# Projection in four overlapped token parts, with first loads of two stages issued one stage earlier

## The chip, the cores and the metric

The kernel runs on one core of a Trainium2 chip. The metric is the device time of one execution in microseconds; a comparison goes by the median of several runs. TensorE (PE in the profile) multiplies, ScalarE (ACT), VectorE (DVE) and GpSimd (POOL) do the rest, and SyncE (SP) issues nearly all DMA transfers in the order of its program.

## The reference, cut to what matters

One inference step of a two-layer decoder over 2048 prompt tokens and 32 sample tokens (8 sequences of 4), width 1024:

```
x          -> pool_layer: rmsnorm, w_in_a, causal window means, w_map_a, silu gate, w_out_a, residual   (x1)
k, v       =  rmsnorm(x1, norm_kv_g) @ w_kv                  # 1024 -> 2048, both are also outputs
q, z       =  rmsnorm(x1, norm_b_g) @ w_in_b                 # 1024 -> 2048
o          =  softmax(q0 k0) v - lam * softmax(q1 k1) v      # 8 heads, ALiBi, causal
y          =  rmsnorm(x1 + (rmsnorm(o) * silu(z)) @ w_out_b)
```
The sample tokens attend to 1024 cached positions as well. Everything is float32.

## The kernel before, in words

The program runs in stages, each a block of its own behind a barrier of all engines: `setup`, `PoolLayer`, `OutLayer` (x1), `project` for tokens 0 to 1023, `project` for tokens 1024 to 2079, `attention` (prompt), `sample_attention`, `last_layer`. Float32 products are made of three matmuls on operands split into a high and a low part (`three`, L295 to L297).

**OutLayer** (L653) splits the weights in eight chunks while TensorE multiplies its first two token blocks; `load_g` (L670) fetches the gated input of block n+2 only when block n has been added up and stored (`step`, L709).

**project** (L808) has eight *units* of weights, each 1024 x 512, in the order v, k, q, z, v, k, q, z; a unit is used by eight *steps* (nine in the second half), one for each 128 tokens, or for a q unit one for each 128 channels by 512 tokens. A step is 24 matmuls. Before the units, the blocks of 128 tokens are normalized: ScalarE squares (L205) and takes the root (L211), VectorE averages (L224) and scales (L230, L233), TensorE turns the block with eight transposes (L253), ScalarE and VectorE split it (`high` L268, `low` L273). Each engine carries out its list in order. The points to follow:

- SP issues the weights of unit u+1 at the start of its list for unit u (L911, `load`, L885), which it reaches after the stores of the last step of unit u-1.
- ScalarE and VectorE split those weights (L949, L981, `split`) at the start of their lists for unit u, ahead of all evictions of unit u. They wait there until the weights have landed.
- Rows of v and k are copied out by VectorE (L986), z goes through Silu on ScalarE (L968), q is split by both (L959, L993).
- A k block is also turned: `turn_keys` (L1024) puts four transposes (L1032) on TensorE two steps later (`LATE = 2`), out of the copied rows; ScalarE and VectorE then split them as well (L959, L993). There are `NR = 3` PSUM banks for these transposes, shared with the norm's, so a turn waits only for the split of the third key block before it (L1030). The products rotate over five PSUM banks, `NS = 5`.

**attention** (L1064) starts with loads of head 0 (L1148): keys and queries in high and low form, in two groups. TensorE waits for the first group before its first score (L1218) and for the second before the second pair of query blocks. GpSimd meanwhile makes the bias tile (L1193 to L1197) that VectorE needs for its first score reduction (L1343). In the profile's rows the output layer's first operand buffers are `early_loads`, the projections' normalized input is `b_x_hi` and `b_x_lo`.

## Time and profile before

| | us |
|---|---|
| median of 3 runs | 3381.88 (3379.08 to 3382.13) |
| profiled execution | 3381.49 |
| its span, first to last instruction | 3379.7 |
| TensorE busy | 3126.8 (93%) |
| VectorE busy | 1581.0 (47%) |
| ScalarE busy | 1188.3 (35%) |
| mean granted TensorE clock | 0.962 of full |

Stages on TensorE by their first and last product: pooling layer until 970, output layer 988 to 1375, first projection 1401 to 1764, second 1792 to 2206, prompt attention 2223 to about 2880, then sample attention and the last layer. Busy time of TensorE is the sum of its matmuls' durations without overlap counted twice; the time between products is what a stage's start or a wait costs. Times of rows are microseconds from the start of the span.

### The profile page before, as it was taken

How to read it: one execution, taken by the hardware profiler on the slowest of the kernel's cores; microseconds unless marked ns; L12 is line 12 of the kernel's file. 1: busy time of each engine (PE TensorE's matmuls, PEld its weight loads, DVE VectorE, ACT ScalarE, POOL GpSimd, SP SyncE). 2: the span in 40 equal slices, each digit the busy share in tenths (PEclk: the TensorE clock that was granted, in tenths of full speed). 3: DMA queues.
4: the chain of work that ended last, by engine and by line, in shares of the span. 5: the costliest groups of instructions: out<-in, count | busy, mean ns of one | idle time of the engine just before them, and what ended most of it. 6: DMA issues, size and time to landing. Idle time of an engine off the chain costs nothing. (4 is left out here: it accounts for less than half of the span.)

```text
span 3379.7 us, 44652 instructions
## 1 busy us (share of the span) xinstructions
PE 3126.8 (93%) x17000; PEld 2582.6 (76%) x17000; DVE 1581.0 (47%) x2673; ACT 1188.3 (35%) x2149; POOL 95.8 (3%) x109
## 2 busy tenths in 40 slices
PE   5999999999978999799988999969999999787598
PEld 4888888889977888588876777749999999543486
DVE  4574655564641111331214312148888888332464
ACT  3333333342320000322113221137777777332222
POOL 0000000000000000000000000010000000000111
PEclk8999999999989999899998999979999999998799
DMA  4434343424233222343324423282445451686453
GB/s 138 137 106 137 106 137 106 139 100 170 83 106 98 90 93 86 120 144 127 128 101 138 138 102 116 93 185 54 111 103 112 103 110 30 263 309 234 168 177 115
DMA packets 249951, 431.96 MB, mean 128 GB/s; under 512 B 20889, under 2 KB 119961, under 8 KB 244217
## 3 DMA queue, kind: packets, MB, share of 16 engines
q1 hardware_dynamic: 249775, 429.59, 40.0%
q8 instruction: 114, 1.87, 0.3%
q14 instruction: 62, 0.50, 0.1%
HBM read 327.30 MB, written 102.95 MB: 127 GB/s over the span
## 5 line engine op out<-in xcount | busy, mean ns | idle before, releaser
L295 PE MATMUL proj_acc<-proj_w_hi,b_x_hi 128*128 128x512 f32 (+1 forms) x832 | 330.0, 397 | 0.0
L297 PE MATMUL proj_acc<-proj_w_hi,b_x_lo 128*128 128x512 f32 (+1 forms) x832 | 326.5, 392 | 0.0
L296 PE MATMUL proj_acc<-proj_w_lo,b_x_hi 128*128 128x512 f32 (+1 forms) x832 | 326.0, 392 | 0.0
L1290 ACT ACTIVATE attn_scores<-attn_scores,attn_lowest 128x1024 f32<-128x1024 f32 (+15 forms) x256 | 307.2, 1204 | 28.8 <-DVE attn_lowest L1343 28.8
L1230 PE MATMUL attn_s<-attn_k_hi_lo,attn_q_lo_hi 128*128 128x512 f32 (+3 forms) x640 | 266.3, 416 | 33.0 <-DMA attn_q_hi_lo<-qT_lo 28.6
L1260 PE MATMUL attn_o<-attn_v,attn_aT 128*128 128x128 f32 x2176 | 295.6, 276 | 1.0 <-ACT attn_aT L1301 1.0
L1260 PEld LDWEIGHTS attn_o<-attn_v,attn_aT 128*128 128x128 f32 x2176 | 279.4, 191 | 10.6 <-ACT attn_aT L1301 1.2
L1343 DVE CUSTOM_DVE_ANT_0 attn_scores<-attn_s,attn_bias 128x1024 f32<-128x1024 f32 (+7 forms) x256 | 216.7, 856 | 151.1 <-PE attn_s L1231 118.3
L295 PE MATMUL pool_acc<-pool_odd_x_hi,pool_wh 128*128 128x272 f32 (+1 forms) x768 | 249.1, 324 | 0.0
L296 PE MATMUL pool_acc<-pool_odd_x_lo,pool_wh 128*128 128x272 f32 (+1 forms) x768 | 248.5, 324 | 0.0
L297 PE MATMUL pool_acc<-pool_odd_x_hi,pool_wl 128*128 128x272 f32 (+1 forms) x768 | 248.3, 323 | 0.0
L295 PE MATMUL outa_acc<-outa_w_hi,outa_g_hi 128*128 128x512 f32 (+1 forms) x544 | 213.9, 393 | 29.2 <-DVE outa_w_lo L764 18.0
L1231 PE MATMUL attn_s<-attn_k_hi_lo,attn_q_hi_lo 128*128 128x512 f32 (+3 forms) x640 | 229.4, 369 | 0.0
L296 PE MATMUL outa_acc<-outa_w_lo,outa_g_hi 128*128 128x512 f32 (+1 forms) x544 | 213.5, 392 | 0.0
L297 PE MATMUL outa_acc<-outa_w_hi,outa_g_lo 128*128 128x512 f32 (+1 forms) x544 | 213.4, 392 | 0.0
L295 PE MATMUL pool_acc<-even_x,pool_wh 128*128 128x512 f32 x512 | 203.6, 398 | 1.4 <-DVE even_x L273 1.4
L297 PE MATMUL pool_acc<-even_x,pool_wl 128*128 128x512 f32 x512 | 201.7, 394 | 0.0
L296 PE MATMUL pool_acc<-even_x,pool_wh 128*128 128x512 f32 x512 | 200.2, 391 | 0.0
L297 PEld LDWEIGHTS proj_acc<-proj_w_hi,b_x_lo 128*128 128x128 f32 (+1 forms) x832 | 151.5, 182 | 40.2
L296 PEld LDWEIGHTS proj_acc<-proj_w_lo,b_x_hi 128*128 128x128 f32 (+1 forms) x832 | 151.9, 183 | 38.4
L295 PEld LDWEIGHTS proj_acc<-proj_w_hi,b_x_hi 128*128 128x128 f32 (+1 forms) x832 | 151.8, 182 | 37.9
L1301 ACT ACTIVATE attn_aT<-attn_t 128x512 f32<-128x512 f32 (+3 forms) x320 | 164.8, 533 | 42.2 <-PE attn_t L1244 39.4
(223 smaller groups left out, 5833.8 us busy)
## 6 DMA issues: line engine op xcount, KB each, us to landing
pool_wu<-in_w_in_a SPq DMA_DIRECT2D x16, 2048.0 KB, 7.8
pool_wz<-in_w_in_a SPq DMA_DIRECT2D x16, 2048.0 KB, 7.7
smp_k_page<-in_cache_k SPq DMA_DIRECT2D x64, 512.0 KB, 5.4
smp_v_page<-in_cache_v SPq DMA_DIRECT2D x64, 512.0 KB, 5.6
pool_wm<-in_w_map_a SPq DMA_DIRECT2D x16, 1024.0 KB, 5.6
early_loads<-gatedT SPq DMA_DIRECT2D x16, 1024.0 KB, 5.9
proj_wst<-in_w_kv SPq DMA_DIRECT2D x8, 2048.0 KB, 9.4
proj_wst<-in_w_in_b SPq DMA_DIRECT2D x8, 2048.0 KB, 8.3
```

The costliest lines, as they stand in the source:

```text
L295: pe.matmul(out, ah, bh, start=first, stop=False)
L296: pe.matmul(out, ah, bl, start=False, stop=False)
L297: return pe.matmul(out, al, bh, start=False, stop=last)
L1230: pe.matmul(out[:, o:o + w], qx[a][:, c, q], keys, start=True, stop=False)
L1231: last = pe.matmul(out[:, o:o + w], qs[a][:, c, q], keys, start=False, stop=True)
L1260: last = pe.matmul(o_ps[r], at[idx % NAT][:, kb % QUAD, :], v[h % 2][:, kb, :], start=kb == 0, stop=kb == n - 1)
L1290: act.activation(part, part, ACT.Exp, scale=-1.0, bias=low[s][:, x:x + 1], accum_out=sums[s][:, i:i + 1]).then_inc(expd, 1)
L1301: act.activation(at[idx % NAT][:, 0:n, :], t_ps[idx % 2][:, 0:n, :], ACT.Copy).then_inc(taken, 1)
L1343: dve.tensor_tensor_reduce(sc[s][:, c, a0:a0 + n], s_ps[idx % 2][:, 0:n], bias[h % 2][:, b0:b0 + n], -SCALE, low[s][:, x - 2:x - 1] if x > ...
```

## The change

There is one `Project` instead of two calls of `project`. Its 2080 tokens come in four parts (512, 512, 512, 544). Each part goes through all eight units, so there are 32 units of four steps (five in the last part), and each of the 32 loads and splits its 2 MB of weights. The normalized input alternates between two buffers: the blocks of part p+1 are normalized during units 1 to 4 (1 to 5 before the last part) of part p, one a unit, with square at step 0, root and scale at step 1, the eight transposes after step 2, `high` and `low` at step 3. The norm has two PSUM banks, the keys one, `key_bank`; a turn of keys waits for the split of the key block just before it. OutLayer fetches its gated input two blocks earlier and issues the first weights (`nxt.load_w`) and the first rows of x1 of the projection. In the last part, at the start of unit 5, SP issues four loads of head 0 (`FirstHead.first_loads`); attention then waits for those and for two smaller ones.

```
+                if i in (3, 4):
+                    sp.wait_ge(g_lo, i - 2)
+                    load_g(sp, i - 1, i - 3, P)
...
+                if ahead:
+                    sp.wait_ge(g_lo, 2 * i + s + 3)
+                    load_g(sp, 2 * i + s + 4, s, ahead)
+                if x_n:
                     sp.wait_ge(out_sem[s], 16 * i + 16)
-                    load_x(2 * i + s + 2, s, n)
-
-            with sp.Fori(0, pairs - 1) as i:
-                step(i, 0, P)
-                step(i, 1, P)
-            step(pairs - 1, 0, rest)
-            step(pairs - 1, 1, 0)
+                    load_x(2 * i + s + 2, s, x_n)
+
+            step(0, 0, P, P, P)
+            sp.wait_ge(w_lo, KC // LK)
+            nxt.load_w(sp, 0)
+            step(0, 1, P, P, P)
+            with sp.Fori(1, pairs - 2) as i:
+                step(i, 0, P, P, P)
+                step(i, 1, P, P, P)
+            step(pairs - 2, 0, P, rest, P)
+            step(pairs - 2, 1, P, 0, P)
+            sp.dma_start(nxt.slots[0][:, :], D["x1"][0:P, :]).then_inc(nxt.row_sem, 16)
+            step(pairs - 1, 0, P, 0, rest)
+            step(pairs - 1, 1, P, 0, 0)
...
+        self.slots, self.x, self.turn_banks = [slot], [], []
+        self.row_sem = m.sem("row_in")
...
+        NS, NR = 5, 3
+        LATE = 2
...
+        self.turn_banks += [m.ps(f"turn{i}", [P, KC // 2, P]) for i in range(2)]
+        key_bank = m.ps("turn_keys", [P, CT, P])
...
+        steps = [(p, u, b) for p in range(PN) for u in range(NUN) for b in range(first_block[p + 1] - first_block[p])]
+        def late_keys(n):
+
+            return n - LATE if n >= LATE and kind(n - LATE) == "k" and whole(n - LATE) else None
...
+        def norm_block(p, u):
+
+            if p + 1 == PN or not 1 <= u <= first_block[p + 2] - first_block[p + 1]:
+                return None
+            return first_block[p + 1] + u - 1
...
+            norm.load(sp, 1)
+            norm.load(sp, 2)
+            self.load_w(sp, 1)
+            norm.load(sp, 3)
+            for n, (p, u, b) in enumerate(steps):
+                w = p * NUN + u
+                if b == 0 and w >= 1 and w + 1 < NWU:
+                    sp.wait_ge(lo, w * KC)
+                    self.load_w(sp, w + 1)
+                if b == 0:
+                    c = norm_block(p, u + 1)
+                    if c is not None:
+                        norm.load(sp, c)
+                if p == PN - 1 and u == NUN // 2 + 1 and b == 0:
+
+                    done = max(d for x, d in t_index.items() if steps[x][0] < p or steps[x][1] < NUN // 2)
+                    for s in range(NR):
+                        sp.wait_ge(t_out[s], 32 * len(range(s, done + 1, NR)))
+                    sp.wait_ge(mm, step_at[PN - 1, 0, 0])
+                    nxt.first_loads(sp)
+                if transposed(n):
+                    store_turned(n)
+                else:
+                    store_rows(n)
+                late = late_keys(n)
+                if late is not None:
+                    store_turned(late)
...
+            def split(w):
+                gain = gains[units[w % NUN][1][3]]
+                act.wait_ge(w_sem[w % 2], 16 * (w // 2) + 16)
+                if w >= 2:
+                    act.wait_ge(mm, step_at[(w - 1) // NUN, (w - 1) % NUN, 0])
...
+            two_ahead(first_block[1], lambda b: norm.moments(act, b), lambda b: norm.high(act, b), lambda: split(0))
+            for n, (p, u, b) in enumerate(steps):
+                w = p * NUN + u
+                if b == 0 and w + 1 < NWU:
+                    split(w + 1)
+                if kind(n) == "z":
+                    r, a = take(act, n)
+                    act.activation(r, a, ACT.Silu).then_inc(taken_act, 1)
+                if transposed(n):
+                    turned_high(n)
+                late = late_keys(n)
+                if late is not None:
+                    turned_high(late)
+                c = norm_block(p, u)
+                if c is not None and b == 0:
+                    norm.square(act, c)
+                if c is not None and b == 1:
+                    norm.root(act, c)
+                if c is not None and b == 3:
+                    norm.high(act, c)
...
+            AHEAD = 2
+            def turn_keys(n):
+                i = k_index[n]
+                wait_taken(pe, n)
+                if i >= 1:
+                    pe.wait_ge(t_lo, t_index[by_k[i - 1]] + 1)
+                    last = pe.transpose(key_bank[:, j, :], res[n % NS][:, j * P:(j + 1) * P], K["ident"][:, :])
+            for n, (p, u, b) in enumerate(steps):
+                w = p * NUN + u
+                if b == 0:
+                    pe.wait_ge(lo, w * KC + KC)
+                if u == 0:
+                    c = first_block[p] + b if p == 0 else first_block[p + 1] - 1
+                    if p == 0 or b == 0:
+                        pe.wait_ge(norm.lo, 2 * c + 2)
+                if n >= NS:
+                    wait_taken(pe, n - NS)
+                w_hi, w_lo = wh[w % 2], wl[w % 2]
+                xh, xl = self.x[p % 2]
+                a = acc[n % NS]
+                rn = tokens(p, b)[1]
+                for k in range(KC):
+                    if transposed(n):
+                        ch = slice(b * P, (b + 1) * P)
+                        last = three(pe, a[:, :], w_hi[:, k, ch], w_lo[:, k, ch], xh[:, k, 0:CN], xl[:, k, 0:CN],
+                                     k == 0, k == KC - 1)
+                    else:
+                        tok = slice(b * P, b * P + rn)
+                        last = three(pe, a[0:rn, :], xh[:, k, tok], xl[:, k, tok], w_hi[:, k, :], w_lo[:, k, :],
+                                     k == 0, k == KC - 1)
+                last.then_inc(mm, 1)
+                late = late_keys(n)
+                if late is not None:
+                    turn_keys(late)
+                if n + AHEAD < first_block[1]:
+                    norm.turn(pe, n + AHEAD)
+                c = norm_block(p, u)
+                if c is not None and b == 2:
+                    norm.turn(pe, c)
...
+    def first_loads(self, sp):
+        HD = self.HD
+        for name, dst, top, bottom in (("kT", self.kk, "hi", "lo"), ("qT", self.qx, "lo", "hi")):
+            for part, rows in ((top, slice(0, HD)), (bottom, slice(HD, P))):
+                src = self.D[f"{name}_{part}"][0:P, :].rearrange("(c p) s -> p c s", c=2)
+                sp.dma_start(f32(dst[rows, :, :]), src).then_inc(self.sem, 16)
...
-            for n in range(6):
-                load_kq(0, n, slice(0, (far + 1) * P) if n < 2 else slice(near * P, (far + 1) * P), begin_in)
-            for n in range(6):
-                if n >= 2:
-                    load_kq(0, n, slice(0, near * P), kq_in[0])
+            for n in (4, 5):
+                load_kq(0, n, slice(near * P, (far + 1) * P), begin_in)
+            for n in (4, 5):
+                load_kq(0, n, slice(0, near * P), kq_in[0])
                 load_kq(0, n, slice((far + 1) * P, S), kq_in[0])
...
-                    pe.wait_ge(begin_in, 96)
+                    pe.wait_ge(head0.sem, 64)
+                    pe.wait_ge(begin_in, 32)
...
+            with ExitStack() as middle:
+                proj = Project(nc, middle, D, K, early, slot, parts, x1_blocks, block_at, gains)
+                head0 = FirstHead(nc, back, D, K, S, kq0)
+                with ExitStack() as inner:
+                    out.ctx, out.m.ctx = inner, inner
+                    out.run(proj)
+                even2 = Memory(nc, middle, "even2").sb("x", [P, size], F32R)
+                proj.run(halves(even2), head0)
+            with ExitStack() as hold:
+                Memory(nc, hold, "hold").sb("kq", [P, 4 * S])
+                attention(nc, D, K, S, H, head0, early, slot)
```
The split, the copies and `turned_low` on VectorE are in the same order as on ScalarE. The rest of the diff gives buffers other places and passes them on.

## Rows read from the trace of the kernel before

**Rows 1.** Waits of TensorE over the whole run (us in total, times, longest):
```profile
PE attn_s L1230 <- DMA attn_q_hi_lo<-qT_lo: 28.6, 2, 16.2
...
PE proj_turn L1032 <- DVE proj_res L986: 0.6, 1, 0.6
```
**Rows 2.** Busy time by stretch: length, then PE, PEld, DVE, ACT, POOL, clock, DMA share, GB/s:
```profile
1764.00:1792.00 28.00, 5.28 (x23) 4.49 (x24) 11.93 (x25) 13.69 (x26) 0.00 (x0) 0.56 0.45 166
1792.00:2206.40 414.40, 414.40 (x1843) 321.44 (x1842) 97.89 (x156) 78.58 (x135) 0.00 (x0) 1.00 0.33 113
```
**Rows 3.** Timeline, TensorE and VectorE, third block of the output layer: start, length, [idle before]:
```profile
1045.44 0.79 PE L295 MATMUL outa_acc<-outa_w_hi,outa_g_hi 128*128 128x512 f32 x1 [11.18 <-DVE outa_g_lo L752]
...
1050.72 0.41 PE L295 MATMUL outa_acc<-outa_w_hi,outa_g_hi 128*128 128x512 f32 x1
...
1033.04 1.23 DVE L757 TENSOR_TENSOR outa_x<-outa_acc,outa_x 128x1024 f32<-128x1024 f32 x1 [12.86 <-PE outa_acc L297]
1043.01 2.29 DVE L752 TENSOR_TENSOR outa_g_lo<-early_loads,outa_g_hi 128x2048 fp32r<-128x2048 f32 x1 [8.75 <-ACT outa_g_hi L735]
```
**Rows 4.** Timeline, all engines, start of the first projection:
```profile
1379.97 0.83 SPq L194 DMA_DIRECT2D proj_x<-x  x2
...
1383.77 1.06 ACT L205 ACTIVATE proj_junk<-proj_x 128x1024 f32<-128x1024 f32 x1 [46.45 <-DMA proj_x<-x]
...
1386.24 0.20 ACT L211 ACTIVATE proj_stats<-proj_stats 128x1 f32<-128x1 f32 x1
...
1387.48 2.82 PE L253 MATMUL proj_turn<-all_ident,proj_x 128*128 128x128 f32 x12 [12.37 <-DVE proj_x L233]
...
1390.11 5.02 ACT L949 ACTIVATE proj_w_hi<-proj_wst,all_gain_kv 128x512 fp32r<-128x512 f32 x8 [2.20 <-DMA proj_wst<-in_w_kv]
...
1397.49 1.28 DVE L273 TENSOR_TENSOR b_x_lo<-proj_turn,b_x_hi 128x512 fp32r<-128x512 f32 x2
...
1401.48 0.78 PE L295 MATMUL proj_acc<-proj_w_hi,b_x_hi 128*128 128x512 f32 x1
```
**Rows 5.** Timeline of TensorE, second projection: one block's eight transposes among products:
```profile
1799.10 1.03 PE L253 MATMUL proj_turn<-all_ident,proj_x 128*128 128x128 f32 x8
```
**Rows 6.** Timelines of VectorE and ScalarE, first k unit:
```profile
1450.16 0.69 DVE L986 COPY proj_res<-proj_acc 128x512 f32<-128x512 f32 x1 [4.75 <-PE proj_acc L297]
...
1466.32 1.88 DVE L986 COPY proj_res<-proj_acc 128x512 f32<-128x512 f32 x3
...
1460.26 5.04 ACT L949 ACTIVATE proj_w_hi<-proj_wst,all_gain_b 128x512 fp32r<-128x512 f32 x8 [20.87 <-DMA proj_wst<-in_w_in_b]
```
**Rows 7.** Timelines of VectorE, SyncE and ScalarE, first q unit:
```profile
1496.94 0.69 DVE L986 COPY proj_res<-proj_acc 128x512 f32<-128x512 f32 x1 [4.17 <-PE proj_acc L297]
...
1514.89 0.69 DVE L993 TENSOR_TENSOR proj_turned_lo<-proj_turn,proj_turned_hi 128x512 fp32r<-128x512 f32 x1 [0.21 <-DVE proj_turned_lo L993]
...
1499.68 0.57 SPq L885 DMA_DIRECT2D proj_wst<-in_w_in_b  x1
...
1507.92 5.03 ACT L949 ACTIVATE proj_w_hi<-proj_wst,all_gain_b 128x512 fp32r<-128x512 f32 x8 [9.94 <-DMA proj_wst<-in_w_in_b]
```
**Rows 8.** Timeline of ScalarE, first z unit:
```profile
1541.94 0.60 ACT L959 ACTIVATE proj_turned_hi<-proj_acc 128x512 fp32r<-128x512 f32 x1 [4.84 <-PE proj_acc L297]
1553.62 5.03 ACT L949 ACTIVATE proj_w_hi<-proj_wst,all_gain_kv 128x512 fp32r<-128x512 f32 x8 [11.08 <-DMA proj_wst<-in_w_kv]
1558.68 1.28 ACT L968 ACT_TABLE_LOAD   x1
1559.97 1.58 ACT L968 ACTIVATE proj_res<-proj_acc 128x512 f32<-128x512 f32 x3
```
**Rows 9.** Timeline, GpSimd and VectorE, start of prompt attention:
```profile
2219.87 1.89 POOL L1197 TENSOR_SCALAR_AFFINE_SELECT attn_bias<-attn_bias 128x2048 f32<-128x2048 f32 x1
...
2224.85 1.23 DVE L1343 CUSTOM_DVE_ANT_0 attn_scores<-attn_s,attn_bias 128x1024 f32<-128x1024 f32 x1 [67.72 <-PE attn_s L1231]
...
2246.03 1.09 DVE L1343 CUSTOM_DVE_ANT_0 attn_scores<-attn_s,attn_bias 128x896 f32<-128x896 f32 x1 [13.39 <-PE attn_s L1231]
```

More of the change, by code:

```diff
@@ L842, in project @@
-        per = [full // 4] * 4 + [1]
-        norm = Norm(m, blocks, K["ident"], lambda b: (xh, xl, b * P), [m.sb(f"x{i}", [P, KC * P]) for i in range(3)],
-                    m.sb("junk", [P, KC * P]), m.sb("stats", [P, 4 * NB]), turn_ps, None, KC * P)
-        AHEAD = 3
-        LATE = 2
-        def keys_at(n):
-            u, b = divmod(n, NB)
-            return (u, b) if n >= 0 and units[u][1][0] == "k" and b < full else None
-        def transposed(u, b):
-            return units[u][1][0] == "q" and b < full
@@ L922, in _, with store_rows @@
-            for s in range(NS if rest else NS - 1):
+            def store_rows(n):
+                p, u, b = steps[n]
+                i, name = units[u][0], kind(n)
+                cols = slice(i * CN, (i + 1) * CN)
+                r0, rn = tokens(p, b)
+                if name in "kv":
+                    dst = D[name + "_prompt"][r0:r0 + rn, cols] if whole(n) else D[name + "_sample"][:, cols]
+                else:
+                    dst = D[name + "_rows"][r0:r0 + rn, cols]
+                wait_taken(sp, n)
+                sp.dma_start(dst, res[n % NS][0:rn, :]).then_inc(out_sem[n % NS], 16)
@@ L923, in _ @@
+            for s in range(NS):
                 sp.wait_ge(out_sem[s], 16 * stores[s])
@@ L999, in after @@
[L999 to L1001 removed]
+                    dve.sem_inc(taken_dve, 1)
             norm.clear(dve)
[L1004 to L1015 removed]
+            two_ahead(first_block[1], lambda b: norm.scale(dve, b), lambda b: norm.low(dve, b), lambda: split(0))
@@ L1070, in attention @@
+def attention(nc, D, K, S, H, head0, early, slot):
     NB = S // P
@@ L1995, in program @@
-        attention(nc, D, K, S, H)
+        gains = [K["gain_kv"], K["gain_b"]]
+        x1_blocks = [(D["x1"][b * P:(b + 1) * P, :], P) for b in range(S // P)] + [(D["x1"][S:NT, :], R)]
+        H = D["cache_k"].shape[2]
+        K["HD"] = D["lambda_q1"].shape[1]
+        size = 2 * KC * part
+        halves = lambda t: [t[:, i * KC * part:(i + 1) * KC * part].rearrange("p (k t) -> p k t", k=KC) for i in range(2)]
+        with ExitStack() as below:
+            even = Memory(nc, below, "even").sb("x", [P, size], F32R)
```

365 lines of the change are left out of this document (158 added, 207 removed).

## The prediction

> **What bounds the kernel now.** I read the page's busy times first: TensorE is busy 3126.8 of 3379.7 us (93%, table above), every other engine under half, so the time can only come out of TensorE's pauses, or go into new ones. Then TensorE's waits: there are few, and they sit where a stage begins. The largest that the change touches is prompt attention waiting for its keys and queries, 28.6 us in two waits; inside a projection there is just one wait of 0.6 us, for a copied key block [rows 1]. The busy times by stretch say the same: the second projection is 414.4 us with TensorE busy in all of them, and the 28.0 us between the two projections hold 5.28 us of work [rows 2]. So the projections are bound by TensorE and the seams by latency. Last I read the timelines of the seams and of one k, one q and one z unit, to see what stands behind each wait, and how much slack the 45 us of an eight-step unit hide. A step takes 5.44 us: the 4.84 us of idle and 0.60 us of work of a q eviction repeat from step to step [rows 8].
>
> **What goes away.**
> (a) Output layer, third block. TensorE idles 11.18 us for the low half of its gated input, then pays for a fallen clock: its next 12 products take 5.28 us (1045.44 to 1050.72) where 12 at full clock take half a step, 2.7. With the input fetched early, VectorE still has to add up the first block (from 1033.04, 1.23 us) and then split (2.29 us), both ahead of TensorE: 1036.6 instead of 1045.4 [rows 3]. I take 8.9 plus 2.5 = 11.4 us; bounds 0 (the two extra 1 MB loads delay the weight chunks as much) and 13.7. The projection's 2 MB and the row block issued by SP here go at nothing: they lie beside 380 us of products, and without that cover would cost some 8 us, as a 2 MB load does below.
> (b) Start of the projection. Before, both row blocks and the weights are issued behind the barrier at 1379.97; the first block is there at 1383.77, the split of the weights starts at 1390.11, block 0 is ready at 1397.49 + 1.28 = 1398.8 and the first product runs at 1401.48. After, block 0 and the weights are there, block 1 is not: issued at 1379.97, there 3.8 us later, squared and rooted by 1385.5, when the split can start, 4.6 us earlier. Only two blocks are turned ahead of the first product, so it starts some 0.7 us behind block 0 instead of 2.7: 2.0 more. 6.6 us; bounds 0 and 21.5 (all from the barrier to the product) [rows 4].
> (c) Seam between the projections. 28.0 us, 1764.0 to 1792.0, are gone, since no block, barrier or first load stands there [rows 2]. But four more blocks are now turned in TensorE's path (three of that seam, one of the first start), eight transposes or 1.03 us each [rows 5]: 28.0 - 4.1 = 23.9 us. The matmuls themselves are as many as before.
> (d) Start of attention. TensorE's first wait does not shrink by its 16 us: GpSimd's bias chain starts behind the same barrier and ends at 2219.87 + 1.89 = 2221.8, and the first reduction, at 2224.85, needs it. That is late next: gain 3.0. The second wait goes whole, for only 1.8 MB of the second group are left, ahead of all other loads: VectorE's idle of 13.39 us becomes some 0.5, gain 12.9 [rows 9]. 15.9 us; bounds 3 and 28.6 [rows 1].
> Sum of gains: 11.4 + 6.6 + 23.9 + 15.9 = 57.8 us.
>
> **What comes in.** 16 more splits of weights: 128 conversions each on ScalarE and VectorE, at 5.04 / 8 = 0.63 us or so [rows 6], 80 us each. By busy time they are hidden, with both engines at about a quarter in the projection [rows 2]. By order they are not. The split of the next weights stands ahead of all evictions of a unit, on both engines, and waits for a load that SP issues when the unit starts. That stall was there before, and it is as long as before; but the unit around it is now 22 us instead of 45, and two things that TensorE waits for now fall inside it. I count from T, the moment at which the last step of the unit before is evicted, and TensorE would reach the end of step j at T + 5.44 j.
> *q unit, keys.* T = 1496.94; the load is issued at 1499.68, split from 1507.92, and the third key block is split (low half) at 1514.89 + 0.69 = T + 18.6 [rows 7]. The fourth key block is turned after step 2, at T + 10.9 + 0.5 = T + 11.4, and with one key bank that waits for the third block's split. Before, three banks made it wait for the first's only. Wait: 7.3 us. Bounds: 0 if the split were over by T + 11, and 10 if the load, with more transfers around it, lands some 3 us later.
> *k unit.* T = 1450.16; split from T + 10.1 to 15.1 on ScalarE; the first key copy ends at 1466.32 + 0.63, T + 16.9 [rows 6], the transposes need it after step 3, T + 16.3: 0.6 us, the wait that before shows once [rows 1]. With a norm block: square 1.2 to T + 16.3, a table load 1.28 [rows 8] to 17.6, root; from root to the transposes took 1.24 us (1386.24 to 1387.48) [rows 4], so T + 18.9 against 16.3 + 0.5 of key transposes: 2.0 us in all.
> *z unit, norm block.* T = 1541.94; split from 1553.62, T + 11.7, to 16.7; table load for Silu to 18.0, Silu of the first step 0.5, square 1.2, Silu of the second 0.5, T + 20.2; table load for the root to 21.5, and 1.24 more: T + 22.8 against T + 16.3 [rows 4, 8]. Wait: 6.5 us.
> *v unit, norm block.* As the k unit, without keys: T + 18.8 against 16.3, 2.5 us.
> *q unit, norm block.* The root is queued behind the fourth key block's split; with that released at T + 19.2 and up to 3 us more for a buffer still being stored, the block is scaled by about T + 23.5 (an estimate), and TensorE, held up by the keys, arrives at 24.6. Nothing.
> Where the trace shows no such wait, its bounds are 0 and the time from T + 16.3 to the end of the chain plus 3 us for a later load.
> Parts 0 to 2 each: k 2.0, q 7.3, z 6.5, v 2.5, k 0.6, q 7.3, z 0 = 26.2; three parts 78.6. The fifth block of the last part adds 0.9 in a k unit. In the last part, five steps let the third key block be split before the long stall, and there is no norm: only 2 x 0.6. Sum 80.7 us.
> *Clock.* Nine of these waits are 6.5 to 7.3 us long. After the 11.18 us of idle the granted clock was at its lower level, 1.2 GHz, and 2.5 us were lost [rows 3]; beside the wait of 0.6 us it stayed at 1.00 [rows 1, 2]. I take 1.5 us each, 13.5 (bounds 0 and 22.5).
> Loss: 94 us. A wait in one unit does not shorten that of the next, since the next load is issued when the next unit starts.
> The rest is at nothing: norm row loads (0.5 MB a unit) and head 0's four 1 MB loads stand on SP behind the weights' load, the next load comes 27 us later, and the DMA engines are a third in use [rows 2]. Without cover the 4 MB would delay one unit by some 5 us.
>
> **Sum.** 3381.5 (the profiled execution; its span 3379.7 and 1.8 around it; the median is 0.4 more) - 57.8 + 94.2 = 3417.9. Forecast: 3418 us, slower by 1.1%.
>
> **The Trainium skill.** The z unit's row shows the Silu starting 1.29 us after its table load started, straight behind it [rows 8]. The Trainium skill, page "ScalarE: Activation LUTs", section "What ACT_TABLE_LOAD costs", gives about 2.66 us for a switch, 1.28 for the load and 1.38 for a drain; the trace agrees with the first part alone. By the page, each of the four switches in front of a norm block's transposes (one in k, two in z, one in v) would add 1.38 us in three parts, 16.6 us in all, and the sum would be 3434. The rows on the clock are above: 5.28 us for 12 products behind an idle stretch. The Trainium skill, page "TensorE: Matmul & The Clock Gate", section "HAM oscillation — how this bites in real kernels", says that a product loop with recurring idle gaps pays for the slow clock at each gap, not once; this trace has only single gaps, so it cannot show it yet.
>
> **Rivals.**
> *A, the waits don't show.* Faster: the weights' load overtakes, because SP reaches it earlier than I count or the transfer is shorter, so splits are over by T + 11. Then only the gains count: 3381.5 - 57.8 = 3324. It decides from a load issued some 7 us earlier. Against: in the q unit SP issues it 2.7 us behind T and the split starts at T + 11.0, in the k and z units at T + 10.1 and 11.7 [rows 6 to 8]; nothing in the change moves the issue within the unit. Chance 0.13.
> *B, only the key bank costs.* The norm blocks' chain is shorter than its parts added up, or the square runs before the split: 6 x 7.3 + 1.2 + 9 of clock = 54, so 3378, no change. For: the pieces come from different places. Against: ScalarE's order is fixed, and it puts the split first. Chance 0.09.
> *C, contention.* With weights at twice the rate and row blocks beside them, each load lands 2 us later, 20 waits: 40 more, 3458. For: the q unit's load already took 8.2 us, with only stores beside it [rows 7]. Against: 0.33 of the DMA's time in use [rows 2]. Chance 0.05.
> *D, table switches cost double where ScalarE is pressed:* Silu and root in turn cost as much again as the 1.28 us of the row, in front of each norm block's transposes: four switches in three parts, 12 x 1.28 = 15.4 us, 3433. Against: the Silu of the z unit follows its load at once [rows 8]. Chance 0.03. It is the page's rule above.
> *E, the early loads do nothing at attention,* for GpSimd's chain and the second group hold as before: only 12.9 us less gain, 3431; inside the forecast's range. Chance 0.04, counted apart.
>
> **Chances and range.** Forecast 0.62, A 0.13, B 0.09, C 0.05, D 0.03, E 0.04, something else 0.04. A measurement of this kernel can tell about 0.2%, 6.8 us. The forecast's own range comes from the clock (-13.5, +9), attention (-12.7, +12.9), and a microsecond either way in 20 waits, taken together 3393 to 3442. For 8 in 10 it has to take in B: 3372 to 3444; A and C are left out. Slower by over 0.2% (above 3388.6): forecast but a hundredth, C, D, E and some of the rest, 0.76. Within: most of B, 0.08. Faster: A and the rest, 0.16.
>
> **What would show it.** Right: in the projection, TensorE waits at the key transposes for the low half of turned keys, some 7 us, six times; at the norm's transposes for the scaled block, about 6.5 us three times, 2 to 3 us six times; a granted clock that falls again and again between the first and the last product of the projection, a stretch of 860 to 880 us. At the output layer's third block 2.3 us of idle. At attention, VectorE's first reduction 3 us earlier behind the barrier, and no 13 us gap. Wrong: TensorE all but gapless in the projection (A); waits for keys only (B); loads landing over 11 us after issue (C); a gap behind table loads (D). The forecast fails if SP issues the weights well before the stores that I put in front of it, or if TensorE does not stop at the fourth key block.

## The result, and the profile of the changed kernel

| | kernel before | changed kernel |
|---|---|---|
| median of the runs, us | 3381.89 (3379.08 to 3382.13, 4 runs) | 3427.74 (3424.3 to 3434.82, 4 runs) |
| profiled span, us | 3379.7 | 3427.2 |

The changed kernel is slower: its time over that of the kernel before is 1.014, with a 95% interval from 1.0123 to 1.0158. That is 46 us, where 36 were forecast. The two spans differ by 47.5 us.

The page of the changed kernel still shows TensorE as the only busy engine (span, then busy us, share, instructions):
```profile
span 3427.2 us, 44871 instructions
...
PE 3148.3 (92%) x17000; PEld 2593.7 (76%) x17000; DVE 1661.0 (48%) x2800; ACT 1280.6 (37%) x2291; POOL 96.0 (3%) x109
```
The surprise of this page is that TensorE's busy time rose by 21.5 us, from 3126.8, though no matmul was added beside the 32 transposes. Its waits (us in total, times, longest) name where it stands still:
```profile
PE proj_turn_keys L1103 <- DVE proj_turned_lo L1065: 44.3, 6, 8.1
PE proj_turn L253 <- DVE proj_x L233: 19.3, 7, 7.0
PE proj_turn L253 <- DVE region_slot L233: 18.5, 4, 8.8
...
PE attn_s L1332 <- DMA attn_q_hi_lo<-qT_lo: 8.6, 1, 8.6
...
PE attn_s L1332 <- DVE attn_lowest L1445: 6.9, 5, 3.7
PE proj_turn_keys L1103 <- DVE proj_res L1058: 3.5, 5, 1.0
PE outa_acc L295 <- DVE outa_g_lo L763: 3.1, 1, 3.1
```
Of the `region_slot` line, 8.8 us are at the start, ahead of the first product. That leaves in the projection 44.3 us in six waits for the low half of turned keys, 3.5 us in five for a copied key block, and 19.3 + 9.7 = 29.0 us in ten for a scaled norm block: 76.8 us, where the two projections of before had 0.6 [rows 1].

Busy times by stretch (length, then PE, PEld, DVE, ACT, POOL, granted clock, DMA share, GB/s), from SP's first row load behind the barrier to the first product, and from there to the end of the last product:
```profile
1370.39:1385.70 15.31, 3.56 (x16) 3.19 (x17) 10.53 (x23) 12.81 (x24) 0.00 (x0) 0.50 0.63 240
1385.70:2266.70 881.00, 804.14 (x3514) 639.03 (x3512) 285.32 (x454) 262.27 (x433) 0.00 (x0) 0.95 0.46 151
```
The same products with nothing in their way take 779.0 us (first experiment below). So 881.0 us are 779.0 of work, 76.8 of waits, and 804.1 - 779.0 = 25.2 us by which the work is slower, at a mean clock of 0.95. The page counts these 25.2 us as busy.

**Where each part ended up.** Marks of the same events in both traces, in us:

| stretch | before | after | difference |
|---|---|---|---|
| up to SP's first row load of the projection | 1379.97 | 1370.39 | -9.6 |
| from there to the first product | 21.5 | 15.3 | -6.2 |
| first to last product of the projection | 805.0 | 881.0 | +76.0 |
| last product of the projection to the first of the sample attention | 687.9 | 671.1 | -16.8 |
| from there to the first product of the last stage | 267.0 | 270.5 | +3.5 |
| from there to the end | 218.4 | 218.9 | +0.5 |

These differences add up to the 47.5 us, within what rounding leaves. The +3.5 is no part of the change. In the twelve other profiled executions of this case that stretch took between 263.5 and 274.3 us, with the same code.

**Output layer.** TensorE at the third block:
```profile
1036.81 0.79 PE L295 MATMUL outa_acc<-outa_w_hi,outa_g_hi 128*128 128x512 f32 x1 [3.06 <-DVE outa_g_lo L763]
...
1039.53 0.63 PE L295 MATMUL outa_acc<-outa_w_hi,outa_g_hi 128*128 128x512 f32 x1
...
1041.18 0.39 PE L295 MATMUL outa_acc<-outa_w_hi,outa_g_hi 128*128 128x512 f32 x1
```
The block comes at 1036.81 instead of 1045.44, 8.6 us sooner [rows 3]: the pause is 8.1 us shorter (3.06 for 11.18), and the layer's first product came 0.6 us earlier already (987.91 for 988.49). But even a pause of 3.06 us is followed by products of 0.63 us. The twelve products up to 1041.18 take 4.37 us; at full clock they would take 2.7. How long the slow clock stays behind this same pause of 3.06 us differs from execution to execution: in eight of the twelve traces that have it the twelve products take 4.2 to 4.4 us, in the other four, that of experiment 1 among them, 5.28, as long as before behind 11.18 us.

**Start of the projection,** all engines:
```profile
1370.39 0.83 SPq L194 DMA_DIRECT2D proj_x<-x  x2
...
1375.70 5.00 ACT L1014 ACTIVATE proj_w_hi<-region_early,all_gain_kv 128x512 fp32r<-128x512 f32 x8
...
1384.11 1.94 PE L253 MATMUL proj_turn<-all_ident,proj_x 128*128 128x128 f32 x8 [7.80 <-DVE even_x L273]
...
1385.70 0.78 PE L295 MATMUL proj_acc<-proj_w_hi,even_x 128*128 128x512 f32 x1
```
The split starts 5.3 us behind SP's load instead of 10.1, and the first product follows it by 10.0 us instead of 11.4 [rows 4].

**First q unit.** Timelines of VectorE, SyncE, ScalarE and TensorE (T is 1436.2, the last eviction of the k unit):
```profile
1436.23 0.69 DVE L1058 COPY proj_res<-proj_acc 128x512 f32<-128x512 f32 x1 [5.46 <-PE proj_acc L297]
...
1438.98 0.58 SPq L842 DMA_DIRECT2D region_early<-in_w_in_b  x1
...
1448.41 5.01 ACT L1014 ACTIVATE proj_w_hi<-region_early,all_gain_b 128x512 fp32r<-128x512 f32 x8 [10.16 <-DMA region_early<-in_w_in_b]
...
1455.37 0.69 DVE L1065 TENSOR_TENSOR proj_turned_lo<-proj_turn_keys,proj_turned_hi 128x512 fp32r<-128x512 f32 x1 [0.21 <-DVE proj_turned_lo L1065]
...
1456.20 1.09 PE L1103 MATMUL proj_turn_keys<-all_ident,proj_res 128*128 128x128 f32 x4 [8.14 <-DVE proj_turned_lo L1065]
...
1459.22 0.63 PE L297 MATMUL proj_acc<-even_x,proj_w_lo 128*128 128x512 f32 x1
1459.65 0.54 PE L295 MATMUL proj_acc<-even_x,proj_w_hi 128*128 128x512 f32 x1
1460.03 0.39 PE L296 MATMUL proj_acc<-even_x,proj_w_hi 128*128 128x512 f32 x1
```
Read it from the bottom up: TensorE stands 8.14 us at the fourth key block's transposes, for the third block's low half, which VectorE has written at T + 19.8 (T + 18.6 in the prediction's count). That write is so late because the split of the next weights stands ahead of it on both engines, and it starts at T + 12.2 because SP asked for these weights at T + 2.8. After the pause, products take 0.63 us until 1459.65.

**First z unit,** ScalarE, and TensorE's wait:
```profile
1482.09 5.02 ACT L1014 ACTIVATE proj_w_hi<-region_early,all_gain_kv 128x512 fp32r<-128x512 f32 x8 [10.05 <-DMA region_early<-in_w_kv]
1487.12 1.28 ACT L1033 ACT_TABLE_LOAD   x1
1488.42 0.60 ACT L1033 ACTIVATE proj_res<-proj_acc 128x512 f32<-128x512 f32 x1
...
1490.55 1.28 ACT L211 ACT_TABLE_LOAD   x1
1491.85 0.20 ACT L211 ACTIVATE proj_stats<-proj_stats 128x1 f32<-128x1 f32 x1
...
1493.09 1.97 PE L253 MATMUL proj_turn<-all_ident,region_slot 128*128 128x128 f32 x8 [6.35 <-DVE region_slot L233]
```
ScalarE does a split, a table load, Silu, the norm's square, Silu, a table load and the root: the root that scales the norm block stands behind six other pieces of work, each straight behind the one before.

**Start of the prompt attention,** SyncE, GpSimd and VectorE:
```profile
2271.83 0.59 SPq L1250 DMA_DIRECT2D attn_q_hi_lo<-qT_hi  x1
...
2279.37 1.89 POOL L1298 TENSOR_SCALAR_AFFINE_SELECT region_early<-region_early 128x2048 f32<-128x2048 f32 x1
...
2281.48 1.23 DVE L1445 CUSTOM_DVE_ANT_0 attn_scores<-attn_s,region_early 128x1024 f32<-128x1024 f32 x1 [41.85 <-POOL region_early L1298]
...
2289.72 1.09 DVE L1445 CUSTOM_DVE_ANT_0 attn_scores<-attn_s,region_early 128x896 f32<-128x896 f32 x1 [0.89 <-PE attn_s L1333]
```
The first reduction comes 14.8 us behind the last product of the projection, where it was 18.4, and it now waits for GpSimd's bias tile. VectorE's gap of 13.39 us ahead of the second group is one of 0.89 [rows 9].

### The profile page after: what moved, and what is told of

It is laid out like the page before. It is cut to its first block and busy times, and to the rows that moved or that the text cites. A ratio compares the mean times of both kernels' runs of the same rounds, so it can differ in the third digit from the quotient of the medians.

```text
span 3427.2 us, 44871 instructions
## 1 busy us (share of the span) xinstructions
PE 3148.3 (92%) x17000; PEld 2593.7 (76%) x17000; DVE 1661.0 (48%) x2800; ACT 1280.6 (37%) x2291; POOL 96.0 (3%) x109
## 5 line engine op out<-in xcount | busy, mean ns | idle before, releaser
L1445 DVE CUSTOM_DVE_ANT_0 attn_scores<-attn_s,region_early 128x1024 f32<-128x1024 f32 (+7 forms) x256 | 216.7, 856 | 112.0 <-POOL region_early L1298 41.9
L295 PE MATMUL proj_acc<-proj_w_hi,proj_odd_x_hi 128*128 128x512 f32 (+1 forms) x448 | 178.1, 398 | 0.0
L297 PE MATMUL proj_acc<-proj_w_hi,proj_odd_x_lo 128*128 128x512 f32 (+1 forms) x448 | 176.9, 395 | 0.0
L296 PE MATMUL proj_acc<-proj_w_lo,proj_odd_x_hi 128*128 128x512 f32 (+1 forms) x448 | 176.7, 394 | 0.0
L1464 DVE SCALAR_TENSOR_TENSOR attn_scores<-attn_scores,attn_coef 128x1024 f32<-128x1024 f32 (+15 forms) x128 | 173.1, 1352 | 4.5
L1346 PE MATMUL attn_t<-all_ident,attn_scores 128*128 128x128 f32 x1088 | 161.6, 273 | 6.0 <-ACT attn_aT L1403 2.7
L1053 DVE SCALAR_TENSOR_TENSOR proj_w_lo<-region_early,all_gain_kv,proj_w_hi 128x512 fp32r<-128x512 f32 x128 | 86.3, 747 | 162.7 <-ACT proj_w_hi L1014 162.7
L1053 DVE SCALAR_TENSOR_TENSOR proj_w_lo<-region_early,all_gain_b,proj_w_hi 128x512 fp32r<-128x512 f32 x128 | 86.3, 747 | 159.7 <-ACT proj_w_hi L1014 159.7
L295 PE MATMUL proj_acc<-proj_w_hi,even_x 128*128 128x512 f32 x384 | 153.3, 399 | 0.0
L297 PEld LDWEIGHTS pool_acc<-pool_odd_x_hi,pool_wl 128*128 128x128 f32 x768 | 144.3, 188 | 11.8
```

The lines of the kernel that those rows point to most:

```text
L295: pe.matmul(out, ah, bh, start=first, stop=False)
L296: pe.matmul(out, ah, bl, start=False, stop=False)
L297: return pe.matmul(out, al, bh, start=False, stop=last)
L1053: dve.scalar_tensor_tensor(out=wl[w % 2][:, k, :], in0=wst[w % 2][:, k, :], scalar=gain[:, k:k + 1], in1=f32(wh[w % 2][:, k, :]), op0=ALU. ...
L1346: last = pe.transpose(t_ps[idx % 2][:, kb % QUAD, :], sc[u % NSC][:, 0, a0 + kb * P:a0 + (kb + 1) * P], K["ident"][:, :])
L1445: dve.tensor_tensor_reduce(sc[s][:, c, a0:a0 + n], s_ps[idx % 2][:, 0:n], bias[h % 2][:, b0:b0 + n], -SCALE, low[s][:, x - 2:x - 1] if x > ...
```

## The experiments

The theory is that the change loses because a unit is now half as long, while the wait for its weights' load, in front of all evictions on two in-order engines, kept its length; TensorE waits for keys and norm blocks that are queued behind it, and every pause costs clock as well. The rival is that the four overlapped parts cost this by themselves (turning in TensorE's path, one key bank, more transfers), whenever the weights come.

**1. Weights asked for one unit earlier.** Changed kernel with
```diff
-                if b == 0 and w >= 1 and w + 1 < NWU:
-                    sp.wait_ge(lo, w * KC)
-                    self.load_w(sp, w + 1)
+                if b == 0 and w + 2 < NWU:
+                    sp.wait_ge(lo, (w + 1) * KC)
+                    self.load_w(sp, w + 2)
```


> The weights of unit w+2 are issued at the start of unit w, where the changed kernel issues those of w+1; nothing else differs, and as many bytes and conversions are made. Theory (the split of the next weights stands in front of all evictions and waits for a load issued only when the unit starts): the 76.8 us of TensorE's waits inside the projection fall to under 5 us, the clock no longer falls there (some 10 us more), so about 3340 us against 3428, and under the kernel before (3382). Rival (the doubled weights' traffic and conversions slow the stage, wherever they are issued): the same bytes cost the same, 3415 to 3430.

Measured: 3322.07 us (3317.81 to 3322.59), over the kernel before 0.9814 (0.9797 to 0.983). TensorE's stretch, and one split of the first q unit with the load that SP then issues:
```profile
1385.62:2164.58 778.96, 778.96 (x3514) 623.82 (x3512) 287.12 (x454) 262.49 (x433) 0.00 (x0) 1.00 0.51 170
...
1436.44 5.01 ACT L1014 ACTIVATE proj_w_hi<-region_early,all_gain_b 128x512 fp32r<-128x512 f32 x8
...
1437.29 0.56 SPq L842 DMA_DIRECT2D region_early<-in_w_kv  x1
```
Not one wait is left between the first and the last product, and the mean clock is 1.00. The split starts with no wait for a transfer. So overlapped parts, one key bank and 170 GB/s make TensorE wait nowhere by themselves: the rival falls, and all 102.0 us that the projection had lost (881.0 - 779.0) come back when the weights are asked for earlier.

**2. The split moved instead of the load.** On ScalarE and on VectorE, in the changed kernel:
```diff
-                if b == 0 and w + 1 < NWU:
-                    split(w + 1)
...
+                if b == 1 and w + 1 < NWU:
+                    split(w + 1)
```
with the new lines behind the evictions, and the norm's root and scaling, of the second step.

> The loads stand where the changed kernel has them; the split of the next weights stands on ScalarE and VectorE behind the evictions of step 1 of the unit instead of in front of step 0. Theory (it is the order that hurts): waits inside the projection go as with the earlier load, since evictions, key splits and the norm no longer stand behind the load; 76.8 us and the clock, about 3340 us. The split then ends at about T + 18, before the next unit at T + 22. Rival (the load's lateness itself holds TensorE, at the first product of a unit): waits of several us for the low weights in each unit, 3400 us or more.

Measured: 3324.96 us (3316.58 to 3332.75), ratio 0.9822 (0.9798 to 0.9845).
```profile
1384.31:2162.83 778.52, 778.45 (x3514) 623.32 (x3512) 286.04 (x454) 263.26 (x433) 0.00 (x0) 1.00 0.51 171
```
Here the weights come as late as in the changed kernel (8.1 to 10.2 us behind an issue that still stands at the unit's start), but what TensorE needs is no longer queued behind them. The two cures reach the same time. The harm is thus neither the late load nor the early place of the split, but the two together.

**3. The load one step earlier only:** as in 1, but issued at the fourth step of the unit before (`b == 3`).

> The weights of unit w+2 are issued at step 3 of unit w, one step (5.4 us) before the changed kernel issues them, and 16 us later than in the kernel that issues them at the unit's start. Theory (each wait is the lateness of the load, carried through a chain of fixed length): every wait inside the projection is 5.4 us shorter; the key waits of 7.4 us become about 2 (12 us in 6), those in z units about 1 (3 us in 3), the others go: 15 us left of 76.8, PE busy near 780 since such short pauses hardly lower the clock, so 3427 - 62 - 20 = 3345 us. Rival (a threshold: the load must be there before the unit, otherwise the evictions block all the same): 3400 us or more.

Measured: 3333.3 us (3327.15 to 3339.53), ratio 0.9849 (0.9831 to 0.9868). A short wait came up in three places, 5.7 us in all; the stretch from the first to the last product is 788.7 us, so another 4.0 went to slower work:
```profile
PE proj_turn L253 <- DVE region_slot L233: 8.8, 1, 8.8
PE proj_turn L253 <- DVE even_x L273: 7.3, 1, 7.3
PE proj_turn_keys L1103 <- DVE proj_turned_lo L1065: 6.1, 5, 3.0
```
The first two lines are those of the start. By the traces SP issues these loads 5.4 to 6.9 us earlier than in the changed kernel, seen from TensorE's start of the unit (3.0 in the first case, 10 to 12 in the five-step units at the end). Rival A's threshold in the prediction was some 7 us. All but 10 of the 102 us are gained.

**4. A second key bank,** paid for with one accumulator:
```diff
-        NS, NR = 5, 3
+        NS, NR, NKB = 4, 3, 2
...
-                if i >= 1:
-                    pe.wait_ge(t_lo, t_index[by_k[i - 1]] + 1)
+                if i >= NKB:
+                    pe.wait_ge(t_lo, t_index[by_k[i - NKB]] + 1)
```


> Two PSUM banks for the turned keys and four for the products instead of one and five. Theory: the waits of the key transposes for the block before (44.3 us in 6) go to 0, but in the three q units with a norm block the root is queued behind the fourth key block's eviction, and its transposes come up at T + 17 with the block scaled only at about T + 24.8: three new waits of about 7 us. Net about 23 us and some clock: 3400 us. Rival (only the key bank costs, the norm is hidden): 3375 us.

Measured: 3397.74 us (3390.78 to 3399.48), ratio 1.0037 (1.0023 to 1.0051). Waits of TensorE:
```profile
PE proj_turn L253 <- DVE proj_x L233: 32.6, 9, 7.4
PE proj_turn L253 <- DVE region_slot L233: 23.6, 5, 8.8
...
PE proj_turn_keys L1103 <- DVE proj_res L1058: 3.2, 4, 1.3
```
The 44.3 us for keys are gone, and 18.4 of them came back in front of norm blocks (29.0 us before, 32.6 + 23.6 - 8.8 = 47.4 now). The prediction's "nothing" for the norm block of a q unit held only because the key wait in the same unit covered it. No product waits for an accumulator in this trace: every pause of TensorE in the projection stands at a turn. Whether one accumulator and one row buffer less delay the other two engines was not separated.

**5. The norm block turned one step later:**
```diff
-                if c is not None and b == 2:
+                if c is not None and b == 3:
```


> The norm's transposes stand after step 3 of a unit instead of after step 2. Theory: each wait for a scaled block (29.0 us in all, 6.0 to 7.0 in a z unit, 0.8 to 2.2 in k and v units) is shorter by a step of 5.4 us: about 3 us are left in three z units, 26 go, and 3 falls of the clock with them: 3397 us. The key waits stay at 44 us. Rival (the key bank alone costs): no change, 3425 to 3430.

Measured: 3380.99 us (3377.28 to 3385.2, 10 runs), ratio 0.9993 (0.9984 to 1.0003): no difference from the kernel before, and 47 us less than the changed one, from which it differs by one digit.
```profile
1386.08:2222.64 836.56, 794.70 (x3514) 633.58 (x3512) 285.52 (x454) 261.83 (x433) 0.00 (x0) 0.97 0.48 159
...
PE proj_turn_keys L1103 <- DVE proj_turned_lo L1065: 38.9, 6, 7.1
...
PE proj_turn L253 <- DVE proj_x L233: 0.6, 1, 0.6
```
The stage is 44.4 us shorter than in the changed kernel, and the sizes are all in view: norm waits 28.4 less, key waits 5.3, copies 1.4, slower work 9.4 (TensorE busy for 794.7 us instead of 804.1). The expectation missed by 16 us. It had 26 us for the norm waits and some 5 for the clock; it left the key waits as they were and priced the clock at half of what came back.

**6. Output layer alone,** on the kernel before: only the early loads of the gated input.

> The kernel before with only the earlier loads of the output layer's gated input. TensorE's pause of 11.2 us before the third block falls to 3.1 us, and the clock still falls after it, as in the changed kernel: 8 to 9.6 us gained, 3373 us. Rival (the extra loads hold up the weight chunks): a new wait in the first 44 us of the layer, and no gain.

Measured: 3375.95 us (3369.24 to 3382.58, 10 runs) beside 3382.32, ratio 0.9982 (0.9971 to 0.9992).
```profile
1035.14 0.79 PE L295 MATMUL outa_acc<-outa_w_hi,outa_g_hi 128*128 128x512 f32 x1 [3.06 <-DVE outa_g_lo L760]
```
A gain of 6.4 us by the medians, with an interval from 2.7 to 9.8. It is there, and rather below the 9.6 us by which the changed kernel's trace is ahead at the next stage.

**7. Attention's early loads undone,** in the changed kernel: all six loads of the first group behind the barrier, and one wait for them.

> The changed kernel with the four early loads of head 0 taken out of the projection and attention's twelve first loads and its two waits as before. By the traces the part gains 12.8 us, by the forecast 15.9: the start's wait of 16 us and the second of 12 us come back, 3440 us. Rival (the early loads only shift the wait to the bias tile): no change, 3428 us. The projection before it should keep its 880.6 us; if it gets shorter, the early loads cost something there.

Measured: 3445.95 us (3442.19 to 3447.63), ratio 1.019 (1.0173 to 1.0207), so the part is worth 18.2 us by the medians. From the last product of the projection to the first of the sample attention it is 689.3 us, against 671.1 with the part and 687.9 before. The projection ahead of it takes 878.2 us instead of 881.0; that can't be put down to the missing loads, since experiment 8, which keeps them, has 878.1.
```profile
PE attn_s L1331 <- DMA attn_q_hi_lo<-qT_lo: 29.0, 2, 15.5
```
The wait of the kernel before, 28.6 us in two, is back [rows 1].

**8. Early loads of the projection undone,** first in the changed kernel, one run:

> The changed kernel with the first weights and the first rows of x1 issued behind the projection's barrier, as before. From the barrier to the first product 15.3 us become about 20: the split waits for the weights, 10.1 us behind the barrier instead of 5.3. Of the 6.2 us that this start gained, 4.8 come from the loads and the rest from turning two blocks instead of three ahead of the first product. Rival: the start is bound by the norm of the second block, and nothing changes.

It took 3423.06 us. The first product came 20.4 us behind SP's load, 5.1 us later than with the part, as expected, but the total is not slower. The stretch of the sample attention explains that: 263.5 us in this execution, the shortest of all, against 270.5 in that of the changed kernel. One run can't price a part of 5 us here. So it was measured again where nothing later waits, on top of experiment 1, five runs each of this and of experiment 1 itself:

> load_ahead with one part of the change taken back: the first normed rows and the first two units' weights of the projection are asked for behind its barrier again, as in the kernel before. Theory (the early loads save the start of the projection 5 to 6.5 us, and with no wait later in the stage nothing can make that up): the first product comes 4.5 to 6.5 us later behind the barrier, with the rest of the stage of the same length, 3327 us. Rival (what the start gains is lost or made up in the first unit, as the one run of the changed kernel without its early loads, 3423.1 us against 3427.7 us, would have it): 3319 to 3323 us.

> The same kernel as load_ahead, run beside the two others of this group so that they can be compared on one chip. Both theories: 3322 us within 3 us, ratio to the kernel before 0.980 to 0.983.

Measured: 3328.87 us (3328.41 to 3330.57), ratio 0.9844 (0.9831 to 0.9857), beside 3324.62 (3322.75 to 3329.65), ratio 0.9832 (0.9819 to 0.9846). The second block's transposes, ahead of which TensorE waits, without and with the early loads:
```profile
1389.69 1.94 PE L253 MATMUL proj_turn<-all_ident,proj_x 128*128 128x128 f32 x8 [9.63 <-DVE even_x L273]
```
```profile
1383.28 1.94 PE L253 MATMUL proj_turn<-all_ident,proj_x 128*128 128x128 f32 x8 [7.78 <-DVE even_x L273]
```
These starts are 6.4 us apart, but 1.3 of them were there when the stage began (SP's first load at 1370.84 and 1369.58). Behind that load the part is worth 5.1 us, to these transposes and to the first product alike (20.4 and 15.3 us); by the medians it is 4.2. The two ratios' intervals overlap, so the part is shown by the rows and only likely by the total.

**9. The bias tile made early,** on top of experiment 1. GpSimd does its iota, product and selection in the projection's block, behind the last split (`pool.wait_ge(lo, NWU * KC)`), and has only a semaphore to raise in attention.

> On top of load_ahead (projection weights asked for one unit earlier, 3322 us): GpSimd makes the prompt attention's first bias tile inside the projection's block, behind the last split of the weights, instead of behind the barrier. Theory (in the changed kernel the first reduction waited for the bias tile, which was ready at 2281.3, while the two loads behind the barrier landed some 4 us earlier and let the products start): the wait for POOL goes, the loads are late next, the first reduction comes 3 to 5 us sooner and the kernel ends 3 to 4 us earlier, about 3318.5, ratio to load_ahead 0.999. Rival (the first group's reductions have slack behind the products, or the two loads bound it alike): no change, 3322.

Measured: 3324.45 us (3321.75 to 3325.26), ratio 0.9827 (0.9814 to 0.9841): the same as experiment 1 beside it. VectorE and TensorE with the early tile, then VectorE without it:
```profile
2174.43 1.22 DVE L1454 CUSTOM_DVE_ANT_0 attn_scores<-attn_s,region_early 128x1024 f32<-128x1024 f32 x1 [37.97 <-POOL region_early L1314]
...
2182.26 0.58 PE L1341 MATMUL attn_s<-first_kq 128*128 128x512 f32 x1 [2.31 <-DMA attn_q_hi_lo<-qT_lo]
...
2184.10 1.09 DVE L1454 CUSTOM_DVE_ANT_0 attn_scores<-attn_s,region_early 128x896 f32<-128x896 f32 x1 [3.08 <-PE attn_s L1342]
```
```profile
2177.81 1.23 DVE L1445 CUSTOM_DVE_ANT_0 attn_scores<-attn_s,region_early 128x1024 f32<-128x1024 f32 x1 [41.85 <-POOL region_early L1298]
...
2185.16 1.09 DVE L1445 CUSTOM_DVE_ANT_0 attn_scores<-attn_s,region_early 128x896 f32<-128x896 f32 x1 [0.58 <-PE attn_s L1333]
```
The last product of the projection ends at 2163.54 with the early tile and at 2163.03 without. Counted from there, the first reduction does come 3.9 us sooner (10.9 instead of 14.8). Then the second group's load is late next: TensorE waits 2.31 us for it, the second group's reduction comes only 1.6 us sooner, and the first product of the sample attention 1.2. The expectation stopped at the first wait and did not ask what stands behind it.

Experiment 1 is as fast as any: 3322.07 and 3324.62 us in its two measurements, with experiments 2 and 9 equal to it within the scatter. It is 1.7 to 1.9% below the kernel before and about 3% below the changed one.

## Why the prediction was right

The forecast was 3418 us, slower; measured were 3427.74. Its main step held: short units around a stall of unchanged length make TensorE wait, and this costs more than all seams give. Term by term, in us:

| step of the prediction | predicted | measured |
|---|---|---|
| (a) output layer | -11.4 | -9.6 |
| (b) start of the projection | -6.6 | -6.2 |
| (c) seam, less four turned blocks | -23.9 | -26.0 |
| (d) start of attention | -15.9 | -16.8 |
| waits for keys in q units | +43.8 | +44.3 |
| all other waits in the projection | +36.9 | +32.5 |
| slower work after them | +13.5 | +25.2 |
| stretches that the change does not touch | 0 | +4.0 |

The total came out closer than its terms. The slower work was 11.7 us above its forecast and the untouched stretches added 4.0, the sample attention's 3.5 among them, which differ from one execution to the next; against that the small waits were 4.4 us below and the gains 0.8 above. So the forecast missed the loss by 10 to 11 us and not by 16, and part of that closeness is luck. The direction does not hang on it.

**The gains.** (a) came 8.6 us sooner, as 8.9 were worked out, with a pause of 3.06 us where 2.3 were expected, because TensorE had begun the layer 0.6 us earlier. The missing part is the clock, where 2.5 us were to come back and 0.9 did (5.28 us for twelve products before, 4.37 after), since the remaining pause lowers it too; in four other traces none came back. (b): both halves were there, the split 4.8 us earlier (4.6 predicted) and 1.4 us between split and product (2.0 predicted). (c) is 805.0 - 779.0 = 26.0 us, with the turned blocks inside; it was measured by the undisturbed stage of experiment 1, not by an edit of its own. Of the 2.1 us above the forecast, 0.6 are the one key wait of before [rows 1]; the rest was not separated. (d): 3.6 us for the first reduction (2.9 of them behind SP's first load there, for the forecast's 3.0) with GpSimd's chain late next, as the prediction named it, and 12.5 for the second group.

**The waits.** The key waits are 8.14, 7.08, 6.77, 7.32, 7.85 and 7.10 us, for 7.3 predicted; the norm waits of the three z units 6.35, 6.01 and 6.98, for 6.5. They are where the count from T put them. The small ones were too high: v units 1.68, 1.85 and 2.21 for 2.5; k units with a norm block 1.0 + 0.9, 1.1 and 2.0 for 2.0 each. Of the second k units of the three parts the first has no such wait and the others 0.72 and 0.33, for 0.6 each; the fifth norm block of the last part, turned in the third of them, waits 0.83 for 0.9. In the last part itself one wait of 0.61 us is left, where 2 x 0.6 were predicted.

**The mis-sized term is the clock,** 25.2 us of slower work for 13.5, above the upper bound of 22.5. The prediction took 1.5 us for each of nine waits, where its one row, behind a pause of 11.18 us, had 2.5. The nine are there (6.0 to 8.1 us long), followed each by 4 to 11 products of 0.63 us or so, a start every 0.43 us instead of 0.23. The transposes run slowly as well (1.97 us for eight instead of 1.03 [rows 5]). Set beside the same matmuls of experiment 1, the forty behind a pause take 1.4 to 2.7 us longer, 2.1 in the mean and 18.6 in all. A tenth place was not foreseen: behind the pause of 2.21 us at 1950.93, and behind two short ones of 0.33 and 0.83 us at 1975.78 and 1977.27, 13 more products were slow, another 3.4 us. The remaining 3 us are no clock: a product lasts 0.39 us and its successor starts 0.23 behind it, so at each of the 21 pauses the last product runs out alone for 0.16 us, which counts as busy too. A step that took 2.5 us for a pause straight from its own row would have given 22.5 and come within 3 us.

The nine long pauses are each followed by slow products. The Trainium skill, page "TensorE: Matmul & The Clock Gate", section "HAM oscillation — how this bites in real kernels", says that recurring gaps pay for the slow clock each time and not once; the trace of the changed kernel agrees. In the z unit the Silu starts at 1488.42, 1.30 us after its load began at 1487.12, and the root at 1491.85, 1.30 us after 1490.55. Both are the load of 1.28 us alone, so rival D fell. The Trainium skill, page "ScalarE: Activation LUTs", section "What ACT_TABLE_LOAD costs", adds a drain of 1.38 us to every switch; neither of these two shows it.

**The other rivals.** A: TensorE was not gapless in the changed kernel, and no load was issued earlier. But its condition, made by hand in experiment 1, gave 3322 us where A's sum was 3324. B: norm blocks did cost, 29.0 us; experiment 4 shows the two costs cover each other. C: transfers took no longer, 8.0 to 10.3 us from issue to landing for 7.7 to 10.4 before; the q unit's split started at T + 12.2 instead of T + 11.0, and at 170 GB/s nothing waits. E: the first reduction did come sooner.

**Left open:** why the stretch of the sample attention varies between 263.5 and 274.3 us from one execution to the next. These 11 us are as wide as the scatter of the runs, but only one execution of each kernel was profiled, so it is not shown that they make it. Also open is whether the missing accumulator costs anything in experiment 4, and why the slow clock stays longer behind the same pause in some executions.

## What to carry to other kernels

When a stage is cut into shorter units, list what happens once a unit and does not shrink with it: here one load of weights, asked for when the unit starts and waited for ahead of all evictions. Either ask for it one unit earlier or queue its consumer behind the work that others need; here both brought the full gain, and one of them belongs in the same change as the cut. Price a pause of the matmul engine as its length plus what its own trace shows of slow products behind such a pause, and where one wait goes, look two waits on, not one.

## What the runs showed of the hardware

- The granted clock falls after pauses much shorter than the one that the trace of before had: products took 0.63 us behind a pause of 3.06 us in the output layer, and in one place behind 2.21 us. Behind other pauses of 1.68 and 1.85 us they took 0.39. Over all traces, each pause of 1.99 us or more between products of the projection was followed by slow products; of three of 1.84 to 1.86 us two were (experiments 4 and 5).
- The price hardly grows with the pause, but it varies: 1.4 to 1.7 us behind the pause of 3.06 us in eight traces and about 3.0 in the four others, 1.4 to 2.7 behind pauses of 6 to 8 us, and 2.6 behind 11.18 us (the first and the last over 24 products).
- A 2 MB load of weights is on hand 9.4 us after its issue (1438.98 to 1448.41; 8.0 to 10.3 over all 32), and 170 GB/s over 779 us made TensorE wait nowhere (experiment 1).
- A switch of ScalarE between Silu and root costs 1.30 us from the start of the table load to the start of the next work, twice in the first z unit.
